# One adaLN panel, from rows to columns: fp32 products with a small matrix of ones, or transposes and a sum on VectorE

## What is computed

```python
mod = jax.nn.silu(c) @ p['ada_w'] + p['ada_b']            # (1 or 8, 9 * 1024)
sh1, sc1, g1, sh2, sc2, g2, sh3, sc3, g3 = jnp.split(mod, N_MOD, axis=-1)
u = _modulate(_rmsnorm(x, p['norm_ff1']), sh1, sc1)       # xn * (1 + scale) + shift
x = x + 0.5 * g1[:, None, :] * _swiglu(u, p['ff1_w1'], p['ff1_w3'], p['ff1_w2'])
u = _modulate(_rmsnorm(x, p['norm_mix']), sh2, sc2)
...                                                        # mLSTM, SSD, merge
x = x + g2[:, None, :] * (merged @ p['w_out'])
u = _modulate(_rmsnorm(x, p['norm_ff2']), sh3, sc3)
x = x + 0.5 * g3[:, None, :] * _swiglu(u, p['ff2_w1'], p['ff2_w3'], p['ff2_w2'])
```

## Time and profile before

| | |
|---|---|
| median of 3 runs | 1449.58 us (1445.29 to 1453.07) |
| the profiled execution's own time | 1454.3 us |
| its span, first to last instruction | 1452.5 us |
| mean granted clock of TensorE | 0.955 of 2.4 GHz |
| TensorE products, records | 9334 |
| TensorE weight loads, busy | 84% |
| VectorE, busy | 53% |
| ScalarE, busy | 42% |
| GpSimd, busy | 10% |
| moved to or from memory | 241.55 MB, mean 166 GB/s |

### The profile page before, as it was taken

The page is one execution under the profiler, slowest core; times in us unless marked ns, Lnnn a source line. Parts: engine busy times, 40 slices in busy tenths (PEclk is TensorE's granted clock), DMA queues, the critical chain, the costliest instruction groups (busy, mean ns, idle before and its releaser), DMA issues. The chain is left out here.

```text
span 1452.5 us, 22917 instructions
## 1 busy us (share of the span) xinstructions
PE 1346.9 (93%) x9334; PEld 1214.2 (84%) x9334; DVE 763.1 (53%) x1308; ACT 611.2 (42%) x1070; POOL 148.1 (10%) x287
## 2 busy tenths in 40 slices
PE   6799999997999987888999999999989889999997
PEld 3599999995998955666999878788989879999997
DVE  0444444334876455554359756855455554555542
ACT  3433333324555434444345564544463244333333
POOL 3000000000320011110013122211100010000000
PEclk9699999997999899999999999999999998999999
DMA  9666666774433277786464253563334444544441
GB/s 264 201 205 203 221 214 184 226 234 139 146 120 91 89 259 251 274 271 190 116 200 148 88 182 108 161 182 117 101 99 138 145 154 136 173 147 136 140 140 57
DMA packets 258607, 241.55 MB, mean 166 GB/s; under 512 B 8399, under 2 KB 242215, under 8 KB 258454
## 3 DMA queue, kind: packets, MB, share of 16 engines
q1 hardware_dynamic: 249198, 211.00, 47.7%
q0 software_dynamic: 8832, 28.91, 5.8%
q10 hardware_dynamic: 472, 0.17, 0.0%
HBM read 209.84 MB, written 30.21 MB: 165 GB/s over the span
## 5 line engine op out<-in xcount | busy, mean ns | idle before, releaser
L1821 DVE TENSOR_TENSOR w_lo<-ring,w_hi 128x1024 fp32r<-128x1024 f32 (+1 forms) x264 | 336.1, 1273 | 523.7 <-ACT w_hi L1306 522.6
L1306 ACT ACTIVATE w_hi<-ring 128x1024 fp32r<-128x1024 f32 (+1 forms) x264 | 289.5, 1097 | 612.6 <-PE bank L664 602.1
L664 PE MATMUL bank<-u_hi,w_hi 128*128 128x320 f32 x1536 | 276.7, 323 | 25.4 <-ACT u_hi L1338 18.9
L664 PEld LDWEIGHTS bank<-u_hi,w_hi 128*128 128x128 f32 x1536 | 238.4, 193 | 44.1 <-issue 27.0
L664 PE MATMUL bank<-u_lo,w_hi 128*128 128x320 f32 x1536 | 262.7, 314 | 0.0
L664 PE MATMUL bank<-u_hi,w_lo 128*128 128x320 f32 x1536 | 259.6, 312 | 0.6 <-DVE w_lo L1821 0.6
L664 PEld LDWEIGHTS bank<-u_lo,w_hi 128*128 128x128 f32 x1536 | 239.7, 193 | 0.0
L664 PEld LDWEIGHTS bank<-u_hi,w_lo 128*128 128x128 f32 x1536 | 236.5, 190 | 0.9 <-DVE w_lo L1821 0.9
L568 POOL TENSOR_TENSOR arena<-arena 128x320 f32<-128x320 f32 x24 | 21.0, 874 | 662.2 <-ACT arena L1318 647.5
L664 PE MATMUL bank<-arena 32*128 32x128 f32 (+6 forms) x600 | 64.5, 382 | 25.2 <-DMA arena<-in_state_mlstm_C 21.5
L664 PEld LDWEIGHTS bank<-arena 32*128 32x128 f32 (+4 forms) x600 | 33.7, 153 | 40.7 <-issue 36.8
(11 more groups left out here) (331 smaller groups left out, 1549.3 us busy)
## 6 DMA issues: line engine op xcount, KB each, us to landing
ring<-in_w_in SPq DMA_DIRECT2D x52, 1024.0 KB, 5.3
ring<-in_ff_w SPq DMA_DIRECT2D x44, 1024.0 KB, 5.4
ring<-in_ada_w SPq DMA_DIRECT2D x36, 1024.0 KB, 7.9
ring<-in_ff_w SPq DMA_DIRECT2D x32, 704.0 KB, 4.6
arena<-in_state_mlstm_C SPq DMA_DIRECT2D x32, 512.0 KB, 4.3
out_s_C<-arena POOLq DMA_DIRECT2D x32, 512.0 KB, 3.9
ring<-in_w_pa SPq DMA_DIRECT2D x8, 1024.0 KB, 7.0
arena<-in_state_ssm SPq DMA_DIRECT2D x32, 256.0 KB, 3.5
```

The lines of the kernel that those rows point to most:

```text
L664: return nc.tensor.matmul(dst, lhs, rhs, start=first, stop=last)
L1306: nc.scalar.activation(w_hi[v.split_no % 2][:, 0:v.kc, :], panel_part(v), ACT.Copy).then_inc(S["hi_done"], 1)
L1821: V.tensor_tensor(w_lo[r][:, 0:v.kc, :], panel_part(v), w_hi[r][:, 0:v.kc, :].bitcast(FP32), ALU.subtract)\
```

## The change

`mod_columns` transposes each half of `mod_row` (128 x 128, with `ident`) in place of the product with `mod_sum`. The PSUM bank then holds 2 x 128 columns: for each of the two halves, 32 g + s runs over the columns. `mod_add` first reduces the four groups on VectorE, 18 sums of four values with a stride of 32 columns, into `mod`, and then adds the bias in place. `mod_sum` and its building are gone, and `ones` is set after `idents_made` is raised.

```diff
-            for m, v in ((ident, 0.0), (mod_sum, 0.0), (ones, 1.0)):
-                ch.inc(nc.gpsimd.memset(m[:], v))
-            ch.settle()
-            keep(ident[:, :], [[-1, 128]], ALU.not_equal, 1.0, 0, 1)
-            for j in range(3):
-                keep(mod_sum[:, :], [[-1, NSEQ]], ALU.not_equal, 1.0, -32 * j, 1)
-            nc.gpsimd.affine_select(out=mod_sum[:, :], in_=mod_sum[:, :], compare_op=ALU.not_equal, fill=1.0, base=-96, pattern=[[-1, NSEQ]],
+            ch.link(nc.gpsimd.memset(ident[:], 0.0))
+            nc.gpsimd.affine_select(out=ident[:, :], in_=ident[:, :], compare_op=ALU.not_equal, fill=1.0, base=0, pattern=[[-1, 128]],
                                     channel_multiplier=1).then_inc(S["idents_made"], 1)
+            ch.link(nc.gpsimd.memset(ones[:], 1.0))
...
                 for j in range(2):
-                    ins = mm(aux[2 + r][:, NSEQ * j:NSEQ * (j + 1)], mod_row[r][:, j * 128:(j + 1) * 128], mod_sum[:, :])
+                    ins = turn(aux[2 + r][:, j * 128:(j + 1) * 128], mod_row[r][:, j * 128:(j + 1) * 128], 128)
                 ins.then_inc(S["mod_turned"], 1)
...
                 dve.wait_ge(S["mod_turned"], p + 1)
-                V.tensor_tensor(mod[:, 2 * p:2 * p + 2, :], aux[2 + p % 2][:, 0:2 * NSEQ].rearrange("p (j s) -> p j s", s=NSEQ),
-                                par[:, 2 * p:2 * p + 2].unsqueeze(2).to_broadcast([128, 2, NSEQ]), ALU.add).then_inc(S["mod_read"], 1)
+                m = mod[:, 2 * p:2 * p + 2, :]
+                ch.link(V.tensor_reduce(m, aux[2 + p % 2][:, 0:256].rearrange("p (j g s) -> p j s g", j=2, g=4)[:, :, 0:NSEQ, :], AX.X, ALU.add))
+                V.tensor_tensor(m, m, par[:, 2 * p:2 * p + 2].unsqueeze(2).to_broadcast([128, 2, NSEQ]), ALU.add).then_inc(S["mod_read"], 1)
```

More of the change, by code:

```diff
@@ L177, in build @@
         last_s = sb("last_s", [64, 64])
-        mod_sum = sb("mod_sum", [128, NSEQ])
         tile_of_head = sb("tile_of_head", [SH, 16])
```

## The result

| | kernel before | changed kernel |
|---|---|---|
| median | 1447.51 us (6 runs, 1442.42 to 1453.07) | 1436.56 us (6 runs, 1434.39 to 1437.28) |
| ratio to before | | 0.9916, interval 0.9896 to 0.9935 |
| ratio, the two kernels measured again | | 0.9908, interval 0.9885 to 0.9930 |
| profiled span | 1452.5 us | 1433.8 us |

A forecast was written before the change was run, and what follows sets the result against it. TensorE, without gaps in the dense stages, was taken as the bound. Dense panels -5.4, head -0.6 and VectorE's reduction +0.27 gave -5.7 us, from 1449.6 to 1443.9 us; the range was 1438 to 1452.5.

The forecast's parts named there:

- The price of a pair: TensorE, dense stages: two transposes cost 0.247 us where a panel's products took 0.48, a gain of 0.23 us per panel.
- the panels that count in up1 and down1: 14 panels in up1 and 6 in down1, of 23 counted at 0.233 us each, 5.4 us in all.
- VectorE's reduction: New reduction from PSUM before each panel's addition: 0.23 us, with 0.04 for the link 0.27 a panel, 9.7 in all.
- its cover in the dense stages: In up1 VectorE idles ahead of nearly every low half of the weights, so the reduction costs nothing there.
- the 0.27 us on the path in the gap after down1: Panel 28's reduction delays the last residual and the sums of squares behind it: 0.27 us lost (0.2 to 0.4).
- the paragraph on POOL: Four selections on the small matrix go, about 1 us; TensorE's first transpose waits for ScalarE anyway, so nothing gained.
- The paragraph on the head: Start of the kernel: first seven panels hidden behind loads; four transposes after the last panel gain 0.6 us (0 to 0.8).
- Rival (b): Low-clock stretches: one unit's length less at 0.50 gives -8.6 us, 1441.0, faster by 0.6%; chance 22%.
- Rival (a): Head, gaps, panels among dense units: clock turns against the change; one more unit after each norm gives 1452.7; 8%.
- Rival (c): Middle, where TensorE waits 21.5 us for matrix memory loads: the 21 panels ahead bring nothing, 1449.1 us; chance 12%.
- (d): Dense panels: VectorE's 0.27 us lands on the path at most of them, a low half late each time, about 1450; 6%.
- (e): A transpose leaves two records after all or waits for the turn from products: no gain per panel, 1449; chance 3%.

The follow-up runs named there:

- after_spare: The changed kernel with an unused tile of 9 columns where `mod_sum` was, so the ring starts at 86080 again: 1441.62 us, ratio 0.9952 to the kernel before.
- before_moved: The kernel before with only `mod_sum` allocated behind `n_t`, so the ring starts 64 bytes lower, at 86016: 1446.21 us against 1449.99, ratio 0.9967.
- turn_twice: The changed kernel with each panel's two transposes issued twice: 1444.69 us, ratio 0.9961 to the kernel before.

## Why the prediction was wrong

**Right.** The price of a pair (0.25 us, 0.247 forecast), that a transpose leaves one record, the panels that count in up1 and down1, VectorE's reduction (226 ns) and its cover in the dense stages, the 0.27 us on the path in the gap after down1. With the ring at its old place the change measures 7.0 us by a ratio whose interval is 0.9933 to 0.9971, and 5.7 us is 0.9961.

**Wrong.** The step that failed is the sentence that closed the paragraph on POOL: "No DMA and no queue of SP moves." No DMA is issued at another point, but all of the loads go to another address. The diff's first line removes a tile of 36 bytes, and I took it as a matter of building constants. It moves the ring by 64 bytes onto a multiple of 256, and that is worth 4.8 us (0.9967, 0.9950 to 0.9985) in the kernel before, where it was tried alone. The two parts add up: 4.8 + 7.0 = 11.8, and 12.2 to 13.3 were measured for both together.

Two smaller steps failed as well. The paragraph on the head counts the first seven panels at nothing, since the panels before them do not push back the products that release the loads; they do, and the head is 2.3 to 3.9 us shorter and not 0.6 (`after_spare`, with the ring at its old place, 0.6 to 1.7). And the gap after down1, forecast 0.27 us longer, is 0.8 to 1.0 us shorter with the transposes alone (7.4 and 7.2 us before, 6.4 in `after_spare`), for the open reason named above. That 7.0 us lie near 5.7 is therefore in part luck: these two terms were missing, and what took about as much back is not known.

**Rival (b)**, the clock in favour of the change with 1441.0 us, would have come nearest with a wrong cause: `before_moved` and `after_spare` differ from their twins in no instruction, and the one gains and the other gives back some two fifths of the whole. The trace looked like (b) all the same: stretches at 0.50 are shorter in the changed kernel. After the second norm they are also shorter in `before_moved` (13.7 us, against 20.5 and 17.1), whose products are the old ones, so there the thin products are not what holds the clock down. For the first norm nothing can be said of `before_moved`: its record of the clock begins at 60.9 us. In the head the clock did stay at 1.00 longer with the transposes, also at the ring's old place, so a part of (b) may be in the 7.0 us.

**Rival (a)**, and the rule of the Trainium skill that stands beside it in the prediction, TensorE: Matmul & The Clock Gate, "Part 4: PE-mode transpose", that transposes do not count for the clock as products do: no loss shows. The mean clock of the two profiles of the changed kernel is 0.962, of before 0.955 and 0.959, of `turn_twice`, with twice the transposes, 0.957.

**Rival (c)**: the memory stage ate nothing that can be seen, and its own spread of 5 us hides anything smaller. **(d)** and **(e)** did not occur.

**The margins.** The forecast started from the median of three runs, 1449.6, and six runs gave 1447.5, 2.1 us less; the range's lower end allowed for 3 us of spread beyond rival (b). With the layout's 4.8 us and 5.7 us the forecast would have been 1439, and from 1447.5 it would have been 1437, beside 1436.56 measured.

## What to carry to other kernels

A tile that goes or comes moves all that is allocated behind it. Ask of every diff that changes an allocation where the targets of the DMAs now start, and put large buffers at a multiple of 256 bytes on purpose; here that was worth 0.3%, where the change itself at the old place brought 0.5%. To tell a layout effect from a compute effect, move the tile alone in the kernel before, and put a dummy in its place in the kernel after. And compare the packets' times before the kernel's: they sorted fourteen profiles without an overlap, where times of the whole kernel overlapped.

## What was not expected of the hardware

- A DMA packet of 512 bytes into SBUF takes 5% more on average (29.3 to 29.6 ns against 27.9 to 28.2) when the ring starts 64 or 128 bytes off a multiple of 256; a quarter of the packets pay for it. Packets of 4096 bytes in the stores, out of an arena that is off the boundary, take 10 to 16% more (183 to 191 ns against 164 to 166). TensorE was 93% busy, and the time still showed the first of the two.
- A fp32 transpose of 128x128 takes half of the time of an fp32 product with 9 columns on the same stationary tile (0.12 against 0.24 us): the product leaves two records of weight loads, the transpose one, and each takes 0.12 us.
- Thrown-away products in the idle time around the norms: after the third norm the dense stage began at a clock of 1.00 in place of 0.50, and the kernel took some 4 us of 1435 less (mean of two ratios on each side).
